# Output projection in four PSUM bank sets, with ten gate products of the first token half ahead of the second half's turn

## The reference

```
y = jnp.concatenate([mixer heads, memory heads], axis=-1) @ w_out     # 1024 x 1024
h = h + rms_norm(y, norm_g[i, 1])
a = rms_norm(h, norm_g[i, 2])
gate, up = jnp.split(a @ ffn_w_in[i], 2, axis=-1)                     # 1024 -> 2 x 2816
f = (jax.nn.silu(gate) * up) @ ffn_w_out[i]
h = h + rms_norm(f, norm_g[i, 3])
```

## Time and profile before

| | us |
|---|---|
| median of 3 runs | 2518.8 |
| the profiled execution | 2516.53 |
| its span, first to last instruction | 2514.5 |
| TensorE busy | 2362.4 (94%) |
| GpSimd busy | 1024.5 (41%) |
| VectorE busy | 1208.7 (48%) |
| ScalarE busy | 935.0 (37%) |

### The profile page before, as it was taken

How to read it: one execution, slowest core, us unless ns; L and a number is a source line. 1 busy time by engine, 2 the same in 40 slices (tenths; PEclk the granted TensorE clock), 3 DMA queues, 4 the chain that set the end, 5 groups by cost and what they waited for, 6 DMA issues and landing times.

```text
span 2514.5 us, 30484 instructions
## 1 busy us (share of the span) xinstructions
PE 2362.4 (94%) x11048; PEld 1938.3 (77%) x11048; DVE 1208.7 (48%) x2185; ACT 935.0 (37%) x1821; POOL 1024.5 (41%) x779
## 2 busy tenths in 40 slices
PE   7999998896899999999989999999869999999998
PEld 6788887684788888788867888877747888887886
DVE  5543444435343344476854333343363344345767
ACT  5421222335232333344644444444443333233443
POOL 4122222263777777200342222212637777771001
PEclk9999999997999999999999999999979999999999
DMA  5111112242233233733431111122323333327334
GB/s 205 34 51 59 43 42 84 81 146 92 88 109 113 93 102 116 282 97 95 155 92 42 40 40 40 40 93 93 134 92 109 105 101 99 115 92 293 96 102 146
DMA packets 100481, 254.73 MB, mean 101 GB/s; under 512 B 21599, under 2 KB 21870, under 8 KB 98286
## 3 DMA queue, kind: packets, MB, share of 16 engines
q1 hardware_dynamic: 100334, 252.80, 30.2%
HBM read 188.00 MB, written 64.77 MB: 101 GB/s over the span
## 4 chain that ended last, share of the span: by engine, by line
PE 84%; ACT 5%; DVE 5%; issue 3%; POOL 3%; DMA 1%; SPq 0%; POOLq 0%; ACTq 0%; DVEq 0%
PE PS L1803 24%; PE PS L1805 24%; PE PS L1804 24%; PE PS L2020 3%; PE PS L2250 2%; PE PS L2030 2%; PE PS L2054 1%; PE PS L2127 1%; POOL TW L705 1%; POOL OPS L681 1%; DMA stage<-in_wpack 1%; PE PS L2206 0%; POOL wlo L639 0%; ACT qbd L1193 0%; PE PS L2138 0%
## 5 line engine op out<-in xcount | busy, mean ns | idle before, releaser
L1803 PE MATMUL PS<-AOP,OPS 128*128 128x512 f32 x1232 | 488.4, 396 | 48.3 <-ACT s L928 12.9
L1805 PE MATMUL PS<-AOP,OPS 128*128 128x512 f32 x1232 | 487.0, 395 | 0.0
L1804 PE MATMUL PS<-AOP,OPS 128*128 128x512 f32 x1232 | 487.0, 395 | 0.0
L639 POOL TENSOR_TENSOR wlo<-stage,whi 128x1024 fp32r<-128x1024 f32 x82 | 202.0, 2468 | 539.8 <-ACT whi L841 539.2
L1803 PE MATMUL PS<-aT,whi 128*128 128x512 f32 (+1 forms) x768 | 335.8, 437 | 5.4 <-DVE aT L1281 3.9
L1803 PEld LDWEIGHTS PS<-AOP,OPS 128*128 128x128 f32 x1232 | 235.6, 191 | 103.6 <-issue 42.0
L1805 PE MATMUL PS<-aT,wlo 128*128 128x512 f32 (+1 forms) x768 | 298.5, 389 | 0.0
L1804 PE MATMUL PS<-aT,whi 128*128 128x512 f32 (+1 forms) x768 | 297.9, 388 | 0.0
L918 ACT ACTIVATE OPS<-TW 128x512 fp32r<-128x512 f32 x176 | 110.8, 632 | 451.1 <-POOL TW L705 408.3
L1805 PEld LDWEIGHTS PS<-AOP,OPS 128*128 128x128 f32 x1232 | 235.7, 191 | 50.4
L1804 PEld LDWEIGHTS PS<-AOP,OPS 128*128 128x128 f32 x1232 | 235.8, 191 | 48.9
(11 more groups left out here) (192 smaller groups left out, 3983.9 us busy)
## 6 DMA issues: line engine op xcount, KB each, us to landing
stage<-in_w SPq DMA_DIRECT2D x88, 512.0 KB, 3.6
stage<-in_wpack SPq DMA_DIRECT2D x82, 512.0 KB, 3.6
hidden_scratch<-HT SPq DMA_DIRECT2D x154, 256.0 KB, 2.2
SRAW<-hidden_scratch SPq DMA_DIRECT2D x154, 256.0 KB, 2.7
BW<-in_w SPq DMA_DIRECT2D x16, 1024.0 KB, 11.6
h_scratch<-Hb SPq DMA_DIRECT2D x24, 512.0 KB, 2.7
Hb<-h_scratch SPq DMA_DIRECT2D x24, 512.0 KB, 6.3
cat_scratch<-OC SPq DMA_DIRECT2D x13, 512.0 KB, 3.0
```

What stands on the lines that cost most here:

```text
L639: pool.tensor_tensor(wlo[:, slot, :], stage[:, slot, :], whi[:, slot, :].bitcast(F32), ALU.subtract)\
L1803: pe.matmul(dst, stat[0], mov[0], start=start, stop=False, skip_group_check=onto)
L1804: pe.matmul(dst, stat[0], mov[1], start=False, stop=False, skip_group_check=onto)
L1805: return pe.matmul(dst, stat[1], mov[0], start=False, stop=stop, skip_group_check=onto)
```

## The change

Four things, the same in both layers.

- The output projection runs in **four sets of four banks**: first token half with output columns 0 to 511, first half with columns 512 to 1023, then the same for the second half. Weight units are packed anew: a unit now holds two channel blocks for one column half. A set's banks are emptied while the next set runs in the other four. A row's sum of squares is made from two halves (`halfsq`), which GpSimd adds.
- In the last set, **`turn(3)` of the first half** is laid between the weight units (four channel blocks behind unit 12, four behind unit 13); the last two units run token tile by token tile.
- Products **1 and 2 of blocks 0 to 4** come first (ten products, two of them per block), `turn_second` stands behind the first four of them instead of behind the first two, and blocks 0 to 4 then have only five products each (7 6 5 4 3). Their gate weights are loaded twice (five DMAs of 512 KB more per layer). The copies of product 1 and the SiLU of blocks 1 to 4 are kept in `Hb`, which is why the residual is reloaded only in block 6.
- The sums of the two halves go to buffers of their own (`S3R`, `S2R`, `S1R`); the low part that GpSimd made (L734) is VectorE's now.

```diff
-OP_SLOT = ((1, 4, 2, 5, 0, 3), (0, 3, 1, 4, 2, 5))
-PAIR_AT = (1, 2)
+OP_SLOT = ((1, 4, 2, 5, 0, 3), (2, 5, 0, 3, 1, 4))
+PAIR_AT = (0, 1)
 PAIR_SLOT = ((0, 3), (1, 4), (2, 5))
 
-A_OF = {"1": 0, "2": 1, "7": 2, "5": 3, "6": 4, "3": 5, "4": 6}
-FIRST_ORDER, ORDER = "1275643", "1627543"
+A_OF = {"1": 0, "2": 1, "7": 2, "3": 3, "6": 4, "5": 5, "4": 6}
+FIRST_ORDER, ORDER = "76543", "1627543"
+NPRE = 5
 OUT_ORDER = "1765432"
 
...
-    return [(j, p) for j in range(KH) for p in (FIRST_ORDER if j == 0 else ORDER)]
+    early = [(j, p) for j in range(NPRE) for p in "12"]
+    return early + [(j, p) for j in range(KH) for p in (FIRST_ORDER if j < NPRE else ORDER)]
 
...
+        W1_UNITS = [2 * j for j in range(NPRE)] + list(range(2 * KH))
+        W1_COUNT = len(W1_UNITS)
...
+        def gated(l, j, which):
+
+            if j < NPRE:
+                return 66 * l + (2 * j + which + 1 if which < 2 else 2 * NPRE + j + 1)
+            return 66 * l + 3 * NPRE + 3 * (j - NPRE) + which + 1
+
+        def s1_of(j):
+            return s1[:, :] if j == 0 or j >= NPRE else Hb[:, j - 1, 0:HALF]
+
+        def sg0_of(j):
+            return sg0[:, :] if j == 0 or j >= NPRE else Hb[:, j - 1, HALF:D]
 
         TW_OF = {"5": 0, "6": 1, "7": 2, "4": 3}
```

SyncE, and ScalarE's tail of the new stretch:

```diff
+            def out_phase(l):
+
+                U, e = U_OUT[l], 16 * l
+                load_units(U + 13)
+                store_h(e)
+                store_h(e + 1)
+                load_units(U + 14)
+                store_h(e + 2)
+                store_h(e + 3)
+                post_loads(2 * l, 0)
+                load_units(U + 16)
+                for m in range(4):
+                    load_w1(l, m)
+                for i in range(3):
+                    store_h(e + 4 + i)
+                load_w1(l, 4)
+                store_h(e + 7)
+                load_gain(2 * l + 1)
...
+                operand_hi(l, 3)
+                gate_out(l, 0)
+                pre_square(s, 1, 3)
+                for q in range(1, 4):
+                    operand_hi(l, q + 3)
+                    gate_out(l, q)
+                raw_second(l)
                 operand_hi(l, 7)
-                act.wait_ge(r_lo, 4 * l + 2)
-                act.wait_ge(r_s, 4 * l + 3)
-                act.activation(AOP[:, 4, 0, :, :], RAWA[:, 0, :, :], ACT.Copy).then_inc(r_hi, 1)
-                act.wait_ge(r_lo, 4 * l + 4)
-                act.wait_ge(r_s, 4 * l + 4)
-                act.activation(AOP[:, 5, 0, :, :], RAWA[:, 1, :, :], ACT.Copy).then_inc(r_hi, 1)
+                hi_second(l)
+                operand_hi(l, 8)
+                gate_out(l, 4)
+                hi_sum(l, "7")
+                operand_hi(l, 9)
+                gate_out(l, 5)
+                operand_hi(l, 10)
+                gate_out(l, 6)
+                hi_sum(l, "6")
+                operand_hi(l, 11)
+                gate_out(l, 7)
+                hi_sum(l, "5")
+                operand_hi(l, 12)
+                gate_out(l, 8)
+                hi_sum(l, "3")
```

TensorE:

```diff
+            def out_unit(l, st, u, tiles=range(TT), ks=None, free=None):
+
...
+                    for i in tiles:
                         if k == 0:
                             for s, v in free(i):
...
+                        rows, f = slice(i * P, (i + 1) * P), slice(HALF * kk, HALF * kk + HALF)
+                        ins = three(PS[:, (D0[l] if fh else 4 - D0[l]) + i, :], (catT[:, th, 0, k, rows], catT[:, th, 1, k, rows]),
+                                    (whi[:, w_slot(n), f], wlo[:, w_slot(n), f]), k == 0, k == KD - 1)
+                        if k == KD - 1:
...
+                    else:
+                        pe.wait_ge(*((f_ea, gated(l, 2, 1)) if j == 4 else (a_lo, a_before(4 * l + 3) + KD)))
+                elif p == "1":
+                    pe.wait_ge(f_ea, gated(l, j - 2, 1))
                 elif j >= 2:
-                    if p == "1":
-                        pe.wait_ge(f_ea, 3 * (g - 2) + 2)
-                    else:
...
             def ffn(l):
                 for q in range(N_IN_FF):
-                    if q == 2:
+                    if q == 4:
...
+                def third(i):
+                    return [(y_late, halves(2 * l, 0, i))]
+
+                def fourth(i):
+                    return [(y_cp, 16 * l + i + 1)]
+
+                t = 4 * l + 3
+                for st, free in enumerate((first, second, third)):
+                    for u in range(4):
+                        out_unit(l, st, u, free=free)
+
+                def turned_free(k):
+                    return [(y_late, halves(2 * l, 1, TT - 1))] if k < 4 else [(a_lo, a_before(t) + k - 3)]
+
+                out_unit(l, 3, 0, free=fourth)
+                turn(t, turned_free, range(4))
+                out_unit(l, 3, 1)
+                turn(t, turned_free, range(4, 8))
+                for i in range(TT):
+                    out_unit(l, 3, 2, (i,))
+                    out_unit(l, 3, 3, (i,))
 
```

More of the change, by code:

```diff
@@ L616, in _ @@
             before_out(1)
-            for th in range(2):
-                load_units(U_OUT1 + KD * (th + 1) + 5)
-                if th:
-                    for u in range(RING):
-                        load_w1(1, u)
-                post(2, th, U_OUT1 + KD if th == 0 else None)
+            out_phase(1)
             ffn(1)
@@ L1302, in post_in_late @@
                 dve.tensor_tensor(Y[:, i, cols], Y1[:, i, cols], gB[:, cols], ALU.mult).then_inc(y_late if half else y_cp, 1)
-            def post_in(s, th):
-                dve.wait_ge(g_ld, 16 * (s + 1))
-                if s % 2 == 0 and th:
-                    dve.wait_ge(t_done, turned(2 if s == 0 else 6))
-                for i in range(TT):
-                    post_in_tile(s, th, i)
             def post_add(s, th, i):
@@ L1333, in post_out, with out_phase @@
                     post_scale(s, th, TT - 1)
+            def out_phase(l):
+                s, t = 2 * l, 4 * l + 3
+                cat_split(l, range(2, 2 * KD))
+                dve.wait_ge(g_ld, 16 * (s + 1))
+                for i in range(TT):
+                    post_half(s, 0, 0, i)
+                for i in range(TT):
+                    post_half(s, 0, 1, i)
+                post_out(s, 0)
+                dve.wait_ge(t_done, turned(2 if s == 0 else 6))
+                for i in range(TT):
+                    post_half(s, 1, 0, i)
+                turn(t, range(6))
+                post_half(s, 1, 1, 0)
+                turn(t, range(6, 7))
+                post_add(s, 1, 0)
+                turn(t, range(7, 8))
+                for i in range(1, TT):
+                    post_half(s, 1, 1, i)
+                    post_add(s, 1, i)
+                    post_scale(s, 1, i - 1)
+                post_scale(s, 1, TT - 1)
             def turn_second(l):
```

601 lines of the change are left out of this document (320 added, 281 removed).

## The result

The changed kernel took 2471.5 us (median of 4 runs, 2468.1 to 2474.9) beside 2518.3 us for the kernel before: ratio 0.9826, 95% interval 0.9810 to 0.9841. It is faster, by 47 us, where 76.4 us were forecast; the predicted 2442 us and the range up to 2470 both lie under it. The profiled execution took 2470.9 us, span 2469.1, which is 45.4 us less than the 2514.5 before.

A forecast was written before the change was run, and what follows sets the result against it. TensorE, busy 94%, bounds the kernel. Layer 1's entry falls from 170.6 to 132.9 us, 37.7 less, layer 2 38.7 less, together 76.4 off 2518.8: predicted 2442 us, own range 2434 to 2452, 8-in-10 range 2430 to 2470.

The forecast's parts named there:

- item 5: Turn of the first half needs the third set's banks empty; late unit 14 weights cost 0.6 us, between 0 and 3.
- item 4: Five handoffs from product 1 to product 2, ScalarE copying between: 1.15 us each, 5.8 us; bounds 4 to 11.5.
- Projection, transposes, ten products: Layer 1 up to the eleventh product: projection 88.9 us, 64 transposes 7.4, ten products at full clock 27.2.
- rival A: The turn starves: unit 14 lands 6.7 us after its issue or later; 5 us per layer, 2452 us; 15%.
- Items 6 and 7: ScalarE's 16 turn copies (9.1 us) and the second half's norm (7 us) are covered by other work.
- Items 8, 9 and 10: Half sums (26 us) come in time; GpSimd's share rises to 87%, still covered; 3.0 us allowed for schedule misses.
- rival B: GpSimd becomes the bound, 2.2 us per operation beside VectorE's sums: 15 us per layer, 2472 us; 14%.
- Behind it both have the same 144 products: From the eleventh product's start both programs have the same products left, 2.72 us each, so only the entry is compared.
- Layer 2's wait for unit 2's low part: Wait of 0.99 us goes, as ScalarE makes that unit's high part earlier; layer 2 saves 38.7 us.
- Rival C: Clock does not hold: all ten early products at half clock, 27.2 us per layer come back, 2497 us; 6%.
- D: Slower than before: clock swings through the five short blocks, up to 35 products per layer at half clock, 2633 us; 3%.

The follow-up runs named there:

- the second profile of the same kernel: The changed kernel measured and profiled once more without any edit: 2473.2 us, ratio 0.9829.
- the pairs: Changed kernel with the early products ordered 1 1 2 2 over pairs of blocks instead of 1 2 1 2: 2472.2 us, ratio 0.9822.
- the experiment with PSUM inputs: Changed kernel with five of VectorE's seven large sums made as four instructions with one PSUM input, results not the needed ones: 2454.5 us, ratio 0.9746.
- the late adds: Changed kernel with the last three sums of a block pair made behind the next block's adds on VectorE: 2465.0 us, ratio 0.9802.
- all edits together: Changed kernel with earlier unit 14 load, squares, copies and operands, GpSimd reordered, later sums, early products paired over blocks: 2448.3 us, ratio 0.9729.
- three more: All edits plus earlier high sum for product 5, block 0's adds before its last sum, earlier unit 12 parts: 2442.1 us, ratio 0.9698.
- With PSUM inputs as well: Kernel with all edits and three more, five large VectorE sums given one PSUM input, results not the needed ones: 2432.1 us, ratio 0.9650.

## Why the prediction was wrong in size

The direction and the mechanism were right: the early products fill the entry, the old waits go. Three steps failed: the turn taken as nearly free (item 5), the engines' work summed engine by engine although VectorE and GpSimd hold each other up and ScalarE's queue passes it on (items 4, 8, 9 and 10), and the stretch behind the eleventh product taken as unchanged. The saving was 45.4 us by the profiles, not 76.4. Against the sum, layer 1 lost 9.9 us before the eleventh product and 4.4 behind it, layer 2 12.8 and 6.6. The 2.7 us that this is more than the 31 missing lie in stages the change doesn't touch, mainly between the layers (686.6 us before, 684.1 now), and are scatter: the second profile of the same kernel has 686.7 there. The 9.9 us of layer 1 are 3.2 at the turn, 1.1 at unit 12, 3.4 at the handoffs and 4.6 of slow clock, less the 3.0 allowed; 0.6 is left. (Each wait is counted with the 0.16 us by which a matmul ends after the next could have been issued, as in item 4.) Point by point, layer 1:

1. *Projection, transposes, ten products* (88.9, 7.4, 27.2): right as amounts at full clock. (The 88.9 takes the wait of 0.41 us off twice, as 562.9 is already the time before it: 0.2 to 0.4 us too little.) But 4.6 us of slow clock stood behind the waits and were in no term: first transpose to first product took 21.6 us instead of 20.0, and from there to the eleventh 43.6 us, of which the work at full clock is 30.9, the waits 8.4, slow clock 3.0, and 1.3 the starts and ends of matmuls around the waits.
2. *Item 4, the handoffs.* The first three measured 1.10, 0.98 and 0.78 us, within the estimate of 1.15. The last two measured 2.19 and 3.30 (4.92 in layer 2). The bounds of 4 to 11.5 us held 8.4 and 10.0. What failed is the reading of the cause: ScalarE's in-order queue stood behind GpSimd, and as the pairs showed, the short handoffs cost nothing. The trace before had this case already. The item says that the handoff was hidden in the other blocks, but the old wait of 6.43 us was block 1's, and ScalarE's copy for it stood behind a split that waited for a combine:

```profile
637.91 0.63 ACT L918 ACTIVATE OPS<-TW 128x512 fp32r<-128x512 f32 x1 [3.74 <-POOL TW L705]
638.96 0.58 ACT L928 ACTIVATE s<-PS 128x512 f32<-128x512 f32 x1
```

3. *Item 5, the turn, is the first step that failed.* 0.6 us was taken, near the lower end; 3.62 and 5.09 us were measured, and 1.12 more at unit 12, which no term had. The weights were issued 2.3 us later than estimated (540.24 for 537.9) and landed 6.8 us after that, like the loads of the residual in the earlier trace rows. The 4.6 us there for projection weights is a median of four; in the same trace, the one unit issued among the residual loads, at 538.13, took 6.7:

```profile
stage<-in_wpack SPq DMA_DIRECT2D x1, 512.0 KB, 6.7
```

That was rival A, given 15%; its price of 5 us per layer was right, since taking the wait away brought the eleventh product 5.1 and 6.4 us forward. What neither had is that the squares need not have stood behind these weights at all.
4. *Items 6 and 7, the turn on ScalarE and the second half's norm*: covered, as forecast; no wait before the first product nor before the second half's transposes.
5. *Items 8, 9 and 10 are the second step that failed.* Each engine's work was summed alone, and their meeting was thrown out with rival B, because the sums end with block 0. They do, but that is where the path runs. By the experiment with PSUM inputs it cost 7 to 8 us per layer in the two stretches, 19 us in all by the time, beside an allowance of 3.0; rival B's upper estimate for a GpSimd operation, 2.2 us, was too low, the measured one is 3.35. The 2.2 was the mean of two unlike ones in the earlier trace rows: the first split took 3.18 us, beside a sum with both inputs in SBUF, the second 1.30, beside steps with an input in PSUM. The Trainium skill, page SBUF — State Buffer (Who interferes with whom), says that a VectorE instruction with two SBUF inputs contends with a GpSimd instruction that reads SBUF. The trace agrees: 3.34 us beside such sums, 1.27 to 1.31 beside those with an input in PSUM.
6. *"Behind it both have the same 144 products"* is the third step that failed. Same products, but five blocks of 13.6 us instead of 19.1 give VectorE less time, and in-order sums of 1.7 us reached the path: 4.4 and 6.6 us, of which 8 together came back when the sums were made later. The condition written down (wrong if this stretch grows beyond 393 us, or the eleventh product comes later than 140) told both.
7. *Layer 2's wait for unit 2's low part*: gone, as forecast.
8. *Rival C* did not come: at the first three handoffs the products behind ran at full clock, as the row of 1688 to 1709 us in the earlier trace rows had shown. It fell to half behind the waits of 2.19 and 3.30 us. The price of C and D is a little high: 5.44 us for a product at half clock doubles 2.72, while twelve matmuls 0.43 us apart take 5.1.
9. *The range.* The bounds named for items 4, 5 and 10 add up to 2432 to 2465 us, wider than the 2434 to 2452 given; the measured time lies outside both.

The parts overlap: by the times, 12 us for the turn, 19 for the meeting of VectorE and GpSimd, 8 for the late adds make 39 us where 31 were missing, and all edits together brought 25, with three more 31. That is 2442.1 us, the forecast's number, but it is no support for the sum: it took edits to all five engines' orders that the forecast did not have, with the eleventh product 8 us earlier and the stretch behind it 10 to 11 us longer than in the sum. With PSUM inputs as well it is 2432 us.

Of the two waits left in the best version, the 2.91 us at the twelfth product is the meeting again: with PSUM inputs it is gone. The 3.14 us at block 5 only falls to 2.35. Open: what in the queues makes that one, and what unit 12's wait is worth.

## What to carry to other kernels

A wait that is closed uncovers the next queue. Before adding up what a fuller TensorE stretch saves, walk each in-order queue and ask of every instruction what may stand in front of it: here a copy of 0.6 us, squares of 0.6 us and an add of 0.7 us were late by 2 to 5 us, each behind something that nobody on the path needed. Where two engines hold each other up, as GpSimd's operations and VectorE's sums of two SBUF inputs do here (1.27 and 2.29 us alone, some 3.35 each side by side), add their times for the stretch in which they meet instead of comparing each with the span. And look at the single rows behind a mean or a median before it becomes a term: the 2.2 and the 4.6 us of this prediction were both the middle of two different cases.

## What was not expected of the hardware

- In the kernel with all edits VectorE and GpSimd take strict turns for 10 us: three sums of 3.38 us against GpSimd operations of 3.34, where alone they take 2.29 and 1.27. Short ones hold each other up too: a hidden sum of 512 elements took 0.69 us or 1.67.
- A load of 512 KB behind four others landed 6.8 us after its issue (540.24 to 547.01); issued ahead of them it took 3.6.
- In the changed kernel half clock followed a wait of 2.19 us before the eighth product of layer 1, and full clock the same wait of 2.19 us in layer 2. Behind waits of 0.8 to 1.1 us between spells of 5.4 us of matmuls the clock stayed at 1.00.
